# Moving loads, scalings and cached-key turns in a hybrid encoder step on one core

## The reference

```python
h = rmsnorm(x, g_mix)
qa, ka, va, qb, kb, vb, lf, ga, gb = in_proj(h, w_in, b_in)
ya = sink_attention(...)   # branch A: 8 query heads, sliding window of 128
yb = fox_attend(...)       # branch B, "fox": 8 heads, all past keys, forget bias
# merge_and_ffn:
merged = sigmoid(ga) * (ya @ w_oa) + sigmoid(gb) * (yb @ w_ob)
x = x + merged @ w_out
h = rmsnorm(x, g_ffn)
a, u = split(h @ w_gu)
x = x + (silu(a) * u) @ w_down
y = rmsnorm(x, g_final)
```

## Time and profile before

| what | value |
|---|---|
| median of three runs | 1594.21 us |
| the profiled execution | 1592.57 us |
| its span, first to last instruction | 1590.8 us |
| TensorE busy | 1558.1 us (98%) |
| VectorE busy | 1033.2 us (65%) |
| ScalarE busy | 702.0 us (44%) |
| mean granted TensorE clock | 0.996 |

### The profile page before, as it was taken

How to read it: one execution, slowest core, us unless ns; L and a number is a source line. 1 busy time by engine, 2 the same in 40 slices (tenths; PEclk the granted TensorE clock), 3 DMA queues, 4 the chain that set the end, 5 groups by cost and what they waited for, 6 DMA issues and landing times.

```text
span 1590.8 us, 26537 instructions
## 1 busy us (share of the span) xinstructions
PE 1558.1 (98%) x10156; PEld 1463.9 (92%) x10156; DVE 1033.2 (65%) x2033; ACT 702.0 (44%) x1376; POOL 202.0 (13%) x356
## 2 busy tenths in 40 slices
PE   8999999999999999998999999999999999999997
PEld 8999999999999999977998999999999999888886
DVE  6655654566656654474674877766777777679864
ACT  6335555566656644352443642222322223434453
POOL 3012221110100110031010000000221122110000
PEclk9999999999999999999999999999999999999999
DMA  7153333434445355878464423322444445766442
GB/s 210 33 161 107 128 115 113 121 104 114 131 117 140 94 170 152 222 243 226 122 200 138 132 75 115 110 82 82 125 145 144 158 150 199 246 216 191 139 137 81
DMA packets 194348, 226.25 MB, mean 142 GB/s; under 512 B 23832, under 2 KB 145210, under 8 KB 193704
## 3 DMA queue, kind: packets, MB, share of 16 engines
q1 hardware_dynamic: 167840, 138.71, 30.6%
q0 software_dynamic: 26384, 85.87, 16.1%
HBM read 166.76 MB, written 57.82 MB: 141 GB/s over the span
## 4 chain that ended last, share of the span: by engine, by line
PE 85%; DVE 7%; DMA 3%; ACT 3%; issue 2%; SPq 0%; DVEq 0%; ACTq 0%; POOLq 0%
PE ps L2492 24%; PE ps L2493 24%; PE ps L2494 23%; PE ps L2558 3%; PE ps L2578 2%; DMA w_raw<-in_w_out_dram 2%; PE ps L2600 1%; PE ps L2601 1%; DVE sprob L1718 1%; PE ps L2615 1%; PE ps L2809 1%; PE ps L2808 1%; DMA w_raw<-in_w_ob_dram 1%; DVE e_lo L2134 1%; PE ps L2655 1%
## 5 line engine op out<-in xcount | busy, mean ns | idle before, releaser
L2492 PE MATMUL ps<-h_hi,w_hi 128*128 128x384 f32 (+1 forms) x816 | 274.1, 336 | 1.3 <-DVE h_lo L1690 1.2
L2494 PE MATMUL ps<-h_hi,w_lo 128*128 128x384 f32 (+1 forms) x816 | 266.5, 327 | 0.0
L2493 PE MATMUL ps<-h_lo,w_hi 128*128 128x384 f32 (+1 forms) x816 | 266.2, 326 | 0.0
L2492 PE MATMUL ps<-t_hi,e_hi 128*128 128x272 f32 x704 | 202.7, 288 | 0.9 <-DVE silu L2149 0.9
L2493 PE MATMUL ps<-t_lo,e_hi 128*128 128x272 f32 x704 | 202.8, 288 | 0.0
L2494 PE MATMUL ps<-t_hi,e_lo 128*128 128x272 f32 x704 | 202.1, 287 | 0.0
L2492 PEld LDWEIGHTS ps<-h_hi,w_hi 128*128 128x128 f32 x816 | 153.4, 188 | 3.4 <-DVE h_lo L1690 1.5
L2492 PE MATMUL ps<-b_hi,e_hi 128*128 128x272 f32 x528 | 152.5, 289 | 2.2 <-DVE silu L2149 1.1
L2493 PEld LDWEIGHTS ps<-h_lo,w_hi 128*128 128x128 f32 x816 | 153.5, 188 | 0.5 <-issue 0.5
L2494 PEld LDWEIGHTS ps<-h_hi,w_lo 128*128 128x128 f32 x816 | 153.2, 188 | 0.0
L2493 PE MATMUL ps<-b_lo,e_hi 128*128 128x272 f32 x528 | 152.1, 288 | 0.0
(11 more groups left out here) (372 smaller groups left out, 3631.2 us busy)
## 6 DMA issues: line engine op xcount, KB each, us to landing
w_raw<-in_w_gu_dram SPq DMA_DIRECT2D x104, 256.0 KB, 3.4
w_raw<-in_w_in_dram SPq DMA_DIRECT2D x68, 256.0 KB, 3.5
zg_d<-stg POOLq DMA_DIRECT2D x28, 544.0 KB, 3.0
act_d<-act POOLq DMA_DIRECT2D x44, 272.0 KB, 2.8
s_d<-s_sum POOLq DMA_DIRECT2D x44, 256.0 KB, 3.4
f_raw<-s_d SPq DMA_DIRECT2D x44, 256.0 KB, 3.0
f_raw<-act_d SPq DMA_DIRECT2D x33, 256.0 KB, 2.7
w_raw<-in_w_out_dram SPq DMA_DIRECT2D x32, 256.0 KB, 3.6
```

Source lines behind the costliest of these rows:

```text
L2492: nc.tensor.matmul(out, l_hi, r_hi, start=start, stop=False)
L2493: nc.tensor.matmul(out, l_hi, r_lo, start=False, stop=False)
L2494: return nc.tensor.matmul(out, l_lo, r_hi, start=False, stop=stop)
```

## The change

It moves work within the programs of four engines and adds or removes none.

- Quarters 1 and 2 of the first pair's cached keys are turned at steps 131 and 132, before at 132 and 133.
- For s = 3, ScalarE casts the last two quarters of `ab_a` ahead of `evac(d + 1)` and all of `ab_b` ahead of `evac(d + 2)`; VectorE normalises first, then scales the fox half, then makes the rests of `ab_a`.
- GpSimd issues the loads of the second group between the gates of the first, and `x1` after the last of these gates.
- The first two blocks of `merge(0)` wait on TensorE for one evacuation each, before both waited for the last.

```diff
         for c in range(4):
-            turns_at[(130, 132, 133, 134)[c]].append(("cache", 0, c))
+            turns_at[(130, 131, 132, 134)[c]].append(("cache", 0, c))
...
             pool.wait_ge(z_pe, N_DENSE)
-            load_x1(0)
             load_gates(0, 4)
             pool.wait_ge(o_ready, N_DUOS + 4)
+            load_outputs(pool, 1, 0)
             pool.dma_start(gffn_row[:, :], g_ffn.broadcast_to([P, D])).then_inc(gains_landed, 16)
-            for j in range(5, KD):
-                load_gates(0, j)
-            load_outputs(pool, 1, 0)
+            load_gates(0, 5)
             pool.wait_ge(sem("ab_lo"), 8)
             load_sums(pool, 1, 0)
-            load_gates(1, 0)
+            load_gates(0, 6)
             for slot in range(2):
                 pool.wait_ge(sem(f"abs_saved{slot}"), 64 * 2)
             pool.wait_ge(sem("ab_scaled"), 8)
             load_outputs(pool, 1, 1)
             load_sums(pool, 1, 1)
+            load_gates(0, 7)
+            load_x1(0)
             for x in range(2):
                 pool.dma_start(rooms[1]["ab_b"][:, x, :, 512:576].bitcast(F32), ots_d[x]).then_inc(sem("ab_landed11"), 16)
+            load_gates(1, 0)
             load_gates(1, 1)
...
                 if s < 3:
                     turned_hi(("cache", s + 1, 2))
+                else:
+                    for k in range(2, 4):
+                        merged_in_hi(0, 0, k)
                 evac(d + 1)
...
-                    for k in range(2, 4):
-                        merged_in_hi(0, 0, k)
+                    for k in range(4):
+                        merged_in_hi(0, 1, k)
                 evac(d + 2)
                 turned_hi(("ots", s))
-                if s == 3:
-                    for k in range(4):
-                        merged_in_hi(0, 1, k)
...
                     merged_in_scale(0, 0, (2, 3))
+                normalise(N_STREAM + s)
+                if s == 3:
+                    merged_in_scale(0, 1, (0, 1, 2, 3))
                     for k in range(4):
                         merged_in_lo(0, 0, k)
-                normalise(N_STREAM + s)
...
                 turned_lo(("ots", s))
                 if s == 3:
-                    merged_in_scale(0, 1, (0, 1, 2, 3))
                     for k in range(4):
                         merged_in_lo(0, 1, k)
...
-                        pe.wait_ge(*((z_evac, N_DENSE) if k < 2 else (part_done, n_pieces)))
+                        pe.wait_ge(*((z_evac, N_DENSE - 1 + k) if k < 2 else (part_done, n_pieces)))
```

## The result

Eight runs of the changed kernel took 1598.65 us in the median (1596.79 to 1600.15), beside a median of 1594.21 us for seven runs of the kernel before; an eighth took 2046.59 us and is left out. The ratio is 1.0027, with an interval of 1.0016 to 1.0039: 4.3 us slower, and told apart from no change. The profiled execution took 1598.51 us, 0.14 under its median, where that of before lay 1.64 under its own. Its span is 1596.7 us, which is 5.9 more than before, at a mean granted clock of 0.993 (before 0.996).

The account below looks back on a forecast made before the run. TensorE, busy 98% of the span, was taken as the bound. The terms -0.3 - 2.4 + (11.0 + 2.9 + 0.5) - (4.1 + 2.9 + 0.5) gave +4.2 us on 1594.21: 1598.4 us, range 1588 to 1603.5.

Parts of the forecast that it names:

- The turns: Cached keys: the 1.34 us wait for quarter 3 goes, about 1.1 us comes at quarter 2; 0.3 us won.
- The fox half: First merge: scalings done earlier let TensorE start the fox half at about 677.65 instead of 680.04; 2.4 us won.
- rival D: Merge's entry: fox loads land too late for the scalings, slower by 6.6 us; chance 0.07 together with rival C.
- The losses of before in `out_first`: Late chunk 43 (4.1 us), its clock fall (2.9) and a later 0.5 us all go: 7.5 us won.
- The order of the queue: GpSimd's new load order costs 11.0 us of lateness, 2.9 of clock and 0.5 for the weights.
- The place and the chain: Gate 7, 12.9 us later, holds up chunk 42's cast; TensorE reaches `out_first` 11.0 us late, largest idle place there.
- rival C: Blocks 5 to 7: SyncE's chunks starve, 41 and 42 later than gate 7, clock falls twice; +10, 1604; 0.07 with rival D.
- the landings of 7 us and more from gate 5 on: Sign on GpSimd's queue: loads from gate 5 on take 7 us and more from issue to landing.
- Gate 7 "over 12": Sign on GpSimd's queue: gate 7 takes over 12 us to landing; within 7 us would mean Rival B holds.
- Rival A: GpSimd's queue drains in 26 to 29 us, gate 7 costs 6.5 to 9.5: 1594 to 1597; chance 0.33.
- Rival B: Lateness spread in pieces under 4 us, clock stays full, or drain of about 24 us: 1590.5, best 1586; chance 0.26.

Follow-up runs that it names:

- e3: The kernel before with only the cached keys' quarters 1 and 2 turned one step earlier: 1592.78 us, ratio 0.9994.
- e1: The changed kernel with GpSimd's load order of before, the other edits kept: 1589.78 us, ratio 0.9972 to the kernel before.
- e4: The changed kernel with weight chunks 39, 40 and 41 read in 2 KB rows instead of 512-byte pieces (wrong weights, times only): 1598.72 us, ratio 1.0029.
- e6: Turns and fox half as changed, GpSimd's order nearly as before, most group 1 loads held until weight chunks are done: 1584.29 us, ratio 0.9942.
- e5: The changed kernel with group 1's fox part loads (2048 KB) and `x1` moved behind the gate of block 7: 1593.05 us, ratio 0.9994.

## Why the prediction was right, and where it failed

The forecast was 1598.4 us, 4.2 over 1594.21; the medians show 1598.65, 4.4 over. By its own terms:

1. **The turns, -0.3.** The wait of 1.34 us went and one of 0.97 stands at quarter 2, for the reason given: 0.37. With the wait for `maxpart` that went too, 530 to 560 has 0.6 us less idle time, in e3 as in the changed kernel.
2. **The fox half, -2.4.** From quarter 3's turn to its start TensorE needs 677.11 - 551.61 = 125.5 us, before 680.04 - 552.12 = 127.9: 2.4 won, as reckoned. The wait of 0.50 for `ab_b` shows that its loads had landed in time, so rival D falls.
3. **The losses of before in `out_first`, -7.5.** All three went: no wait, and full clock from 734 on. But e1 shows that they do not go by themselves: with GpSimd's order of before the wait is still 4.33 us.
4. **The order of the queue, +14.4 gross.** The trace shows 13.7 us of waits and 3.1 of clock, 16.8. This term was too small by 2.4. The drain itself was well reckoned: 6400 KB in 30.5 us, and from gate 4 at 697.3 to gate 7 at 728.6 it took 31.3.
5. **The place and the chain: wrong.** The step that failed is "gate 7 is 12.9 us later, so TensorE comes to `out_first` 11.0 us late". Gate 7 landed about where it was forecast (727.3, with the 2.4 us of the shift taken off 729.7), but by then TensorE had lost its time: the idle time came at blocks 6 and 7, and what ended it was not a gate but weight chunks 40 and 41. I had looked at the queue into which the loads were moved and left 0.5 us for its effect on the other one. From "SyncE's chunks come in shorter rows in this stage and take less from the queue" I drew only that GpSimd's queue drains faster. The same fact means that SyncE's chunks are the ones that starve: 0.62 MB beside 5.01.

This is rival C's mechanism (SyncE's chunks starve, the clock falls twice), one or two chunks earlier than it said, and at 16.8 us gross, between the forecast's 14.4 and C's 20.3.

**Where the hit is luck.** Both chains hang on the same drain. Gate 6 and chunk 40 land within a moment of each other (716.4 and 716.3), and e4 shows that without the starving the late gates alone give 1598.72. So the direction and rough size of the cost follow from the bytes in the queue, as reckoned. That the median came out within 0.3 us does not. In the trace the terms are -0.6 - 2.4 - 7.5 + 16.8 = +6.3, the spans differ by 5.9, and the forecast was +4.2: 1.7 too small. Set against e1, the whole miss is the order: it costs 1596.7 - 1588.0 = 8.7 us in the spans, where the forecast's terms give 14.4 - 7.5 = 6.9, while the rest wins 2.8 against 2.7. The median hid this, because I had added to the sum the 1.64 us by which before's profiled execution lay under its median, as if it belonged to every kernel. The changed kernel's lay 0.14 under. The two errors, 1.7 and 1.5, cancel. The profile of before was of one of its better executions: beside the experiments 37 others took 1591.92 to 1596.29 us, at mean clocks from 0.997 down to 0.994.

Of the list of what would show it, these came as said: the wait at quarter 2, the `ab_b` wait, the landings of 7 us and more from gate 5 on (10.3, 13.1, 7.9), the absent wait at chunk 43, and the full DMA share, to 738. Gate 7 "over 12" (7.9) did not come, since its issue waits for block 5 to be gated, and the stall put that off to 720.72, when the last loads ahead of it were about to land (723.7 and 726.4). In e4 it was issued at 714.07 and took 16.8 us, to 730.9: the drain sets its landing, whatever the issue. ScalarE waited for gates 5 and 7 but not for 6, and the largest wait was not at the start of `out_first`.

Rival A wanted the queue to drain in 26 to 29 us; 31.3 excludes it. Rival B wanted a drain of about 24 us or the late pieces each to be under 4 us; the piece of 10.9 us excludes it.

On the share of the queues: if the engines take one packet from each in turn, the 1024 packets of a chunk of 512 KB bring some 1024 x 3.9 KB of GpSimd's with them, 4.5 MB in all. At the 254 GB/s that moved in 694.2 to 716.4 that is 17.7 us by estimate. The second half of chunk 40 took 21.6, and the 3.8 us in which SyncE's queue moved no packet are most of the difference. With 2 KB rows the same reckoning gives 256 x 5.9 KB, about 6 us, and with as long a start about 10; e4's chunk took up to 10.7. Why nothing of a chunk moves in the first 4 us is not shown. The Trainium skill (DMA: Bandwidth & Descriptors, "Queues, rings and completion order") says that each engine takes turns between the queues that have work, a packet at a time. By that rule a queue of short packets gets few bytes beside one of long packets, and the trace agrees, with the packets that the profile counts: from 702 to 714 they are 770 of SyncE's beside 771 of GpSimd's, and 0.38 MB against 2.92. Beside the long rows of e4 the counts are less even (98 of GpSimd's and 145 of SyncE's in 698 to 701, 241 and 139 in 701 to 705), so there the rule is not shown.

What stays open: the 0.4 us between the terms' +6.3 and the spans' +5.9. And no run here has the weights in long rows and the bulk paced together.

## What to carry to other kernels

When loads are moved "into idle time" on one DMA queue, reckon the landing of what another queue moves at the same time, above all where that one has short pieces: a backlog on one queue is paid for by the small transfers of the other. Reckon the issue times anew too, since a stall moves whatever waits behind it. Pace bulk that nobody needs soon by the progress of what is needed (e6, 4.8 us better than the same kernel without it), and when the removal of one cause wins nothing (e4), look whether the wait has only changed its name. When a forecast is summed from the trace of one execution, compare it with the trace of the new kernel first: a median can hit by the scatter of the execution that was profiled.

## What the runs showed of the hardware

- A 512 KB chunk in 512-byte pieces landed 21.6 us after its issue beside a full GpSimd queue, in 2 KB rows 10.7 us. For the first 3.8 us none of its packets moved. A gate of 512 KB on GpSimd's own queue landed in 4.4 us with nothing ahead of it, and in 10.3 and 13.1 behind group 1's loads.
- From 702 to 714 the two queues moved packets one for one, though GpSimd's were eight times as long: 182 and 182 in 706 to 710, 0.76 MB and 0.09. When GpSimd's ran out in e5, SyncE's queue went from 64 packets in a microsecond to 547.
- The total rate at full share depended on what moved: 254 GB/s in 694.2 to 716.4 with group 1's outputs and sums and some gates, and as little as 203 in one window above; 420 with `x1`.
- The granted clock was still 1.00 in 708 to 710, after TensorE had stopped at 707.8; it was 0.91 in 710 to 712, then 0.50, and back at 1.00 only in 722 to 724 although TensorE worked again from 718.68. A second idle place of 2.81 us that ended at 728.77 was followed by 0.50 again (730 to 732), while one of 2.20 us in e6 and one of 2.26 us in before were not. The length of the idle place does not settle it: one of 2.03 us in e4, which ended at 721.46, was followed by 0.50 (723 to 726).
